# A diffusion block on one core: waits for row copies a block later, vector steps a slice sooner, and the down stage's first slices begun with the other token tile

## The chip, the cores and the metric

The kernel runs on one core of a Trainium2 chip. The metric is the device time of one execution in microseconds (us), as a median over runs. The core has a matrix engine (TensorE; PE in the profile, with its weight loads apart as PEld), a vector engine (VectorE, DVE), an activation engine (ScalarE, ACT), GpSimd (POOL) and SyncE (SP). They run their own instruction streams side by side and meet at semaphores. Matmul results lie in PSUM, eight banks of 128 x 512 floats; everything else lies in SBUF.

## What is computed

Two layers of a diffusion backbone over 256 latent tokens of width 2048. Layer 0 mixes tokens by attention (with 256 context tokens), layer 1 by a two-dimensional Fourier transform. Each mixer is followed by a squared-ReLU MLP of inner width 8192, and each sub-layer is normalised, shifted and scaled, and gated, by vectors that are products of SiLU(c) with a 2048 x 12288 matrix:

```python
mod_lat = (silu_c @ ada_w[i] + ada_b[i])[:, None, :]
sh1, sc1, g1, sh2, sc2, g2 = jnp.split(mod_lat, N_MOD, axis=-1)
...
x = x + g1 * o_lat
x = x + g2 * sq_relu_mlp(modulate(rms_norm(x, norm_mlp_g[i]), sh2, sc2), mlp_w1[i], mlp_w2[i])
...
return rms_norm(x, final_norm_g)
```

All is float32. The change touches the MLP of both layers and the modulation vectors that are worked out beside it.

## The kernel before

**Precision.** Each weight tile is split in two parts that TensorE reads in one pass each: ScalarE copies `raw` to `w_hi` (`split_hi`, line 496), VectorE subtracts to get `w_lo` (`split_lo`, line 887). A *slice* is 128 x 1024 weights. Four slices lie ready (`SPLIT`); the split of slice s + 4 waits until TensorE has finished slice s (`slice_done`), and VectorE's part comes behind ScalarE's (`hi_ready`, then `lo_ready`). SyncE loads pairs of slices, 1 MB each, into a ring of three.

**Up.** 16 blocks of 8 slices (s = 0 to 127). `up_slice` runs 8 pairs of matmuls for each slice, one of 512 columns (line 1574) and one of 256 (line 1576). A block fills four PSUM banks, odd blocks banks 4 to 7, even blocks banks 0 to 3. Behind a block ScalarE copies one half of its banks to `u` (`b_half`, line 804), then VectorE adds the other half (`add_halves`, line 1327), which sets `ab_ready` and frees the banks; then ScalarE makes the squared ReLU.

**Down.** 128 slices, two to each of 64 row tiles k of `mlp_w2`. `rows_slice` multiplies a slice with token tile 0 (banks 4 to 7) and then token tile 1 (banks 0 to 3), two banks and so 6 matmuls for each (lines 1530, 1533, 1534). Its first slices wait for the last block's `add_halves(15)`, since block 15 used banks 4 to 7.

**Modulation vectors.** VectorE builds vector v in 16 steps, `ada_step(v, t)`, each a 128 x 2048 multiply-add into `ada_sum` (line 912; the first, line 910, only multiplies). GpSimd loads the 1 MB that a step reads (line 466) into a ring of two, once the step two before is done. In layer 0's up stage vectors 3, 4 and 5 are built. `step_slices` says behind the split of which slice of VectorE's loop each step stands. At the slices of `turns` TensorE sums the result over the partitions: for vectors 3 and 5 (slices 42 and 122) with `lay_rows` (line 1506), for gates, that is vector 4 (slice 82) and, in layer 1, vector 9 (slice 106), with `turn_row` (line 1522), four matmuls into the four banks that the running block doesn't use. A gate needs its bias first (`add_bias`, line 920, a one-partition add that sets `biased`); ScalarE copies the four banks to `g_row` (line 649, `row_ready`), and TensorE waits for that before it goes on with the next slice.

All order is written by hand: each engine's stream is its program text, with the waits where they stand.

Of the kernel before, what the change touches and what calls it, by code (L numbers as in the profile page):

```python
# [30 lines left out]
KT = D // P  # L31
# [3 lines left out]
FT = D_FF // P  # L35
# [19 lines left out]
ROWS = {0: 0, 4: 1, 6: 2, 9: 3}  # L55
COLS = {3: 0, 5: 1, 7: 2, 8: 3}
LAID = {3: 6, 5: 7}
UP_STEPS = {0: (3, 4, 5), 1: (9,)}
# [4 lines left out]
def step_slices(l):  # L63

    if l == 0:
        return {(0, 44, 85)[j] + (12 * t) // 5: (v, t) for j, v in enumerate(UP_STEPS[0]) for t in range(KT)}
    return {6 * t: (9, t) for t in range(KT)}


def turns(l):  # L70

    return {42: 3, 82: 4, 122: 5} if l == 0 else {106: 9}
# [83 lines left out]
def layer_block(nc, x, c, ctx_in, c_ctx, ada_w, ada_b, norm_mix_g, norm_mlp_g, w_qkv, q_g, k_g, w_o,  # L156
# [144 lines left out]
    row_ready = sem("row_ready")  # L301
# [3 lines left out]
    lo_ready = sem("lo_ready")  # L305
    slice_done = sem("slice_done")
# [34 lines left out]
    ab_ready = sem("ab_ready")  # L341
# [3 lines left out]
    ulo_ready = sem("ulo_ready")  # L345
# [1037 lines left out]
    def _(pe):  # L1383
# [152 lines left out]
        def rows_slice(first, k, half):  # L1536
# [5 lines left out]
                    ins = rows_bank(s, k, tt, nb, k == 0, False)  # L1542
            ins.then_inc(slice_done, 1)

        def rows_last(first, k0):

            for tt in range(2):
                for nb in range(4):
                    pe.wait_ge(lo_ready, first + 2 * k0 + 3 + nb // 2)
                    rows_bank(first + 2 * k0 + nb // 2, k0, tt, nb, False, False, 1 if tt == 1 and nb == 2 else 0)  # L1550
                    ins = rows_bank(first + 2 * k0 + 2 + nb // 2, k0 + 1, tt, nb, False, True, 2 if tt == 1 and nb == 3 else 0)
                    if tt == 0 or nb < 3:
                        ins.then_inc(bank_full, 1)
            ins.then_inc(slice_done, 1)
# [31 lines left out]
        for i in range(8):  # L1586
# [3 lines left out]
            for k in range(2):  # L1590
                for tt in range(2):
                    f = 2 * i + k
                    ins = nc.tensor.transpose(ps[:, i % 4, k * T + tt * P:k * T + (tt + 1) * P], xn_in[:, tt, f * P:(f + 1) * P],
                                              ident[:, :])
# [114 lines left out]
        for l in range(2):  # L1709
# [102 lines left out]
            for blk in range(16):  # L1812
                if blk == 1:
                    pe.wait_ge(hT_ready, 2 * (8 * q + 8))
                if blk >= 2:
                    pe.wait_ge(ab_ready, 16 * l + blk - 1)
                for p in range(8):
                    if blk == 0:
                        if 1 <= p < 5:
                            turn_pair(p + 3)  # L1820
                        pe.wait_ge(hl_ready, 8 * q + p + 1)
                    up_slice(l, blk, p)
                    t = turns(l).get(8 * blk + p)
                    if t is not None:
                        pe.wait_ge(ab_ready, 16 * l + blk)
                        if t in ROWS:
                            turn_row(t, range(4), 4 * ((blk + 1) % 2))
                            pe.wait_ge(row_ready, 4 * ROWS[t] + 4)
                        else:
                            lay_rows(t, 4 * ((blk + 1) % 2))  # L1830
                    t = picks(l).get(8 * blk + p)
                    if t is not None:
                        pick_cols(t, 4 * ((blk + 1) % 2))
                if l == 0 and blk in (5, 15):
                    pe.wait_ge(mod_ready, COLS[(3, 5)[blk // 15]] + 1)

            first = 2 * P_DOWN[l]
            for k in range(FT - 2):
                for half in range(2):
                    if half == 0 and k % 2 == 0:  # L1840
                        pe.wait_ge(ulo_ready, 32 * l + k // 2 + 1)
                    if k == 0:
                        pe.wait_ge(ab_ready, 16 * l + 16)
                    rows_slice(first, k, half)
            pe.wait_ge(ulo_ready, 32 * l + 32)
            rows_last(first, FT - 2)
# [48 lines left out]
```

## Time and profile before

| | us |
|---|---|
| median of 3 runs | 2121.84 |
| lowest and highest | 2119.29, 2124.86 |
| the profiled execution | 2124.03 |
| its span in the trace | 2122.2 |

All positions in the text are microseconds from the start of that span. Layer 0's up stage lies at about 510 to 884 and its down stage behind it; layer 1's up stage lies at about 1389 to 1758. "Idle" of an engine is time before an instruction in which it did nothing; the profile puts it down to the instruction or transfer that ended it.

### The profile page before, as it was taken

How to read it: one execution, taken by the hardware profiler on the slowest of the kernel's cores; microseconds unless marked ns; L12 is line 12 of the kernel's file. 1: busy time of each engine (PE TensorE's matmuls, PEld its weight loads, DVE VectorE, ACT ScalarE, POOL GpSimd, SP SyncE). 2: the span in 40 equal slices, each digit the busy share in tenths (PEclk: the TensorE clock that was granted, in tenths of full speed). 3: DMA queues.
4: the chain of work that ended last, by engine and by line, in shares of the span. 5: the costliest groups of instructions: out<-in, count | busy, mean ns of one | idle time of the engine just before them, and what ended most of it. 6: DMA issues, size and time to landing. Idle time of an engine off the chain costs nothing.

```text
span 2122.2 us, 25347 instructions
## 1 busy us (share of the span) xinstructions
PE 2034.3 (96%) x10468; PEld 1649.6 (78%) x10468; DVE 1344.2 (63%) x1351; ACT 979.0 (46%) x1275; POOL 109.3 (5%) x196
## 2 busy tenths in 40 slices
PE   4999979999999999999999999999999999999997
PEld 3677745567888878788888888878888887888886
DVE  2456876447877867677658867876656544545455
ACT  4433554435554554444444444354544554444443
POOL 1111001000000000000000000000000000000000
PEclk8999989999999999999999999989999999999999
DMA  9798548585988979688669826967777555555653
GB/s 369 267 337 328 197 171 314 197 309 182 356 315 311 357 274 350 217 317 327 247 216 354 344 70 238 365 202 245 243 252 238 188 172 178 197 198 188 211 196 119
DMA packets 150924, 538.90 MB, mean 254 GB/s; under 512 B 8437, under 2 KB 9621, under 8 KB 113301
## 3 DMA queue, kind: packets, MB, share of 16 engines
q1 hardware_dynamic: 116816, 329.73, 44.2%
q0 software_dynamic: 31744, 201.34, 25.6%
q10 hardware_dynamic: 2248, 6.21, 0.8%
q8 instruction: 83, 1.36, 0.3%
q14 instruction: 33, 0.26, 0.0%
HBM read 535.15 MB, written 2.10 MB: 253 GB/s over the span
## 4 chain that ended last, share of the span: by engine, by line
PE 89%; DVE 5%; DMA 3%; ACT 2%; issue 1%; POOL 0%; DVEq 0%; SPq 0%; ACTq 0%; POOLq 0%
PE ps L1574 22%; PE ps L1576 11%; PE ps L1530 11%; PE ps L1533 11%; PE ps L1534 11%; PE ps L1388 5%; PE ps L1389 5%; PE ps L1390 5%; PE ps L1449 1%; PE ps L1429 1%; DVE ada_sum L912 1%; DMA spare<-in_ada_w 1%; PE ps L1700 1%; PE ps L1652 1%; DMA c_rows<-in_ctx 1%
## 5 line engine op out<-in xcount | busy, mean ns | idle before, releaser
L887 DVE TENSOR_TENSOR w_lo<-raw,w_hi 128x1024 fp32r<-128x1024 f32 x624 | 759.5, 1223 | 585.8 <-ACT w_hi L496 585.7
L496 ACT ACTIVATE w_hi<-raw 128x1024 fp32r<-128x1024 f32 x624 | 658.1, 1059 | 902.5 <-PE ps L1534 380.2
L1574 PE MATMUL ps<-hh,w_hi 128*128 128x512 f32 x2048 | 723.4, 399 | 4.6 <-DVE hh L1208 3.3
L1576 PE MATMUL ps<-hh,w_lo 128*128 128x256 f32 x2048 | 573.5, 280 | 0.0
L1574 PEld LDWEIGHTS ps<-hh,w_hi 128*128 128x128 f32 x2048 | 386.1, 189 | 101.9 <-issue 4.8
L1530 PE MATMUL ps<-w_hi,hh 128*128 128x512 f32 x1024 | 400.0, 391 | 5.0 <-DVE u L1327 2.6
L1533 PE MATMUL ps<-w_lo,hh 128*128 128x512 f32 x1024 | 399.8, 390 | 0.0
L1534 PE MATMUL ps<-w_hi,hh 128*128 128x512 f32 x1024 | 399.5, 390 | 0.0
L1576 PEld LDWEIGHTS ps<-hh,w_lo 128*128 128x128 f32 x2048 | 387.6, 189 | 0.0
L912 DVE SCALAR_TENSOR_TENSOR ada_sum<-ada_raw,silu,ada_sum 128x2048 f32<-128x2048 f32 x98 | 229.8, 2345 | 3.6 <-DMA ada_raw<-in_ada_w 3.6
L1530 PEld LDWEIGHTS ps<-w_hi,hh 128*128 128x128 f32 x1024 | 192.9, 188 | 46.1 <-issue 6.0
L1534 PEld LDWEIGHTS ps<-w_hi,hh 128*128 128x128 f32 x1024 | 193.1, 189 | 40.4
L1533 PEld LDWEIGHTS ps<-w_lo,hh 128*128 128x128 f32 x1024 | 193.0, 189 | 39.8
L1388 PE MATMUL ps<-w_hi,hh 128*128 128x512 f32 x448 | 195.6, 436 | 16.2 <-DVE hh L1006 9.6
L1389 PE MATMUL ps<-w_lo,hh 128*128 128x512 f32 x448 | 177.6, 397 | 0.0
L1390 PE MATMUL ps<-w_hi,hh 128*128 128x512 f32 x448 | 177.1, 395 | 0.0
L466 POOL DMA_DIRECT2D ada_raw<-in_ada_w x132 | 69.8, 529 | 1230.0 <-DVE ada_sum L912 738.1
L1388 PEld LDWEIGHTS ps<-w_hi,hh 128*128 128x128 f32 x448 | 85.9, 192 | 60.4 <-issue 37.1
L1389 PEld LDWEIGHTS ps<-w_lo,hh 128*128 128x128 f32 x448 | 86.0, 192 | 23.3 <-issue 7.7
L1390 PEld LDWEIGHTS ps<-w_hi,hh 128*128 128x128 f32 x448 | 85.6, 191 | 19.0
L1352 DVE TENSOR_TENSOR hh<-u,hh 128x512 fp32r<-128x512 f32 x64 | 43.4, 683 | 0.0
L1327 DVE TENSOR_TENSOR u<-ps,u 128x1024 f32<-128x1024 f32 x32 | 39.0, 1218 | 6.5 <-ACT u L804 6.5
(180 smaller groups left out, 1320.4 us busy)
## 6 DMA issues: line engine op xcount, KB each, us to landing
raw<-in_mlp_w SPq DMA_DIRECT2D x256, 1024.0 KB, 5.3
ada_raw<-in_ada_w POOLq DMA_DIRECT2D x151, 1024.0 KB, 5.8
spare<-in_ada_w POOLq DMA_DIRECT2D x32, 1024.0 KB, 7.5
raw<-in_attn_w_qkv SPq DMA_DIRECT2D x24, 1024.0 KB, 9.9
raw<-in_attn_w_o SPq DMA_DIRECT2D x16, 1024.0 KB, 7.2
raw<-in_fourier_w_o SPq DMA_DIRECT2D x16, 1024.0 KB, 5.6
g_row<-in_ada_w POOLq DMA_DIRECT2D x9, 1024.0 KB, 10.0
x_tm<-in_x ACTq DMA_DIRECT2D x2, 1024.0 KB, 7.6
```

Source lines behind the costliest of these rows:

```text
L466: pool.dma_start(ring(vector_slot(i)), ada_v[lay][m, i % KT]).then_inc(ada_in[vector_slot(i)], 16)
L496: act.activation(w_hi[:, s % SPLIT, :], raw[:, piece % RAW, s % 2, :], ACT.Copy).then_inc(hi_ready, 1)
L887: nc.vector.tensor_tensor(w_lo[:, s % SPLIT, :], raw[:, s // 2 % RAW, s % 2, :], w_hi[:, s % SPLIT, :].bitcast(F32), ALU.subtract).then_in ...
L912: ins = nc.vector.scalar_tensor_tensor(sum_of(v)[:, :], ring(slot), col, sum_of(v)[:, :], ALU.mult, ALU.add)
L1388: mm(dst, w_h, m_h, start=start, stop=False, skip_group_check=True)
L1389: mm(dst, w_h, m_l, start=False, stop=False, skip_group_check=True)
L1390: return mm(dst, w_l, m_h, start=False, stop=stop, skip_group_check=True)
L1530: ins = mm(bank_of(tt, nb), h_hi[:, k % KT, tok], w_hi[:, s % SPLIT, cols], start=start, stop=False)
L1533: mm(bank_of(tt, nb), h_hi[:, k % KT, tok], w_lo[:, s % SPLIT, cols], start=False, stop=False)
L1534: return mm(bank_of(tt, nb), h_lo[:, k % KT, tok], w_hi[:, s % SPLIT, cols], start=False, stop=stop)
L1574: mm(ps[:, bank, :].rearrange("p (a t) -> p a t", a=2), w_hi[:, s % SPLIT, w], hh[:, k, :, :], start=(k == 0), stop=False, skip_group_chec ...
L1576: ins = mm(ps[:, bank, 0:T], w_lo[:, s % SPLIT, w], h_hi[:, k, :], start=False, stop=(k == KT - 1), skip_group_check=True)
```

## The change

Three edits. `step_slices`: vector 4 begins a slice sooner (43 for 44) at the same spacing, so that its last step stands at slice 79 and not 80; vector 5 begins a slice sooner (84 for 85) and takes a step every 11/5 slices for 12/5, so that its last step stands at slice 117 and not 121. In up, TensorE's wait for `row_ready` moves from behind `turn_row` to the start of the next block. In down, the first two slices (k = 0) are done by a new function, `rows_first`: token tile 1 of both slices first, which only needs block 14's banks, then the wait for `add_halves(15)`, then token tile 0 of both. No work is added or taken away.

```diff
-        return {(0, 44, 85)[j] + (12 * t) // 5: (v, t) for j, v in enumerate(UP_STEPS[0]) for t in range(KT)}
+        return {(0, 43, 84)[j] + ((12, 12, 11)[j] * t) // 5: (v, t) for j, v in enumerate(UP_STEPS[0]) for t in range(KT)}
...
+        def rows_first(l, first):
+
+            pe.wait_ge(ulo_ready, 32 * l + 1)
+            pe.wait_ge(ab_ready, 16 * l + 15)
+            for tt in (1, 0):
+                if tt == 0:
+                    pe.wait_ge(ab_ready, 16 * l + 16)
+                for half in range(2):
+                    if tt == 1:
+                        pe.wait_ge(lo_ready, first + half + 1)
+                    for nb in (2 * half, 2 * half + 1):
+                        ins = rows_bank(first + half, 0, tt, nb, True, False)
+                    if tt == 0:
+                        ins.then_inc(slice_done, 1)
...
+                for t in range(8 * blk - 8, 8 * blk):
+                    if turns(l).get(t) in ROWS:
+                        pe.wait_ge(row_ready, 4 * ROWS[turns(l)[t]] + 4)
...
                             turn_row(t, range(4), 4 * ((blk + 1) % 2))
-                            pe.wait_ge(row_ready, 4 * ROWS[t] + 4)
...
-            for k in range(FT - 2):
+            rows_first(l, first)
+            for k in range(1, FT - 2):
                 for half in range(2):
                     if half == 0 and k % 2 == 0:
                         pe.wait_ge(ulo_ready, 32 * l + k // 2 + 1)
-                    if k == 0:
-                        pe.wait_ge(ab_ready, 16 * l + 16)
```

In what follows `up_slice`'s two lines, 1574 and 1576, are 1589 and 1591 in the changed kernel.

VectorE in layer 0's up stage, around the end of vector 4; line 1327 is `add_halves(9)`, 912 the last steps, 920 the bias. Before:

```order
L887 TENSOR_TENSOR w_lo<-raw,w_hi 128x1024 x2
L1327 TENSOR_TENSOR u<-ps,u 128x1024
L887 TENSOR_TENSOR w_lo<-raw,w_hi 128x1024
L912 SCALAR_TENSOR_TENSOR ada_sum<-ada_raw,silu,ada_sum 128x2048
L920 TENSOR_TENSOR ada_sum<-ada_sum,g_row 1x2048
L887 TENSOR_TENSOR w_lo<-raw,w_hi 128x1024 x5
L910 TENSOR_SCALAR ada_sum<-ada_raw,silu 128x2048
```

The same place in the changed kernel:

```order
L887 TENSOR_TENSOR w_lo<-raw,w_hi 128x1024 x3
L912 SCALAR_TENSOR_TENSOR ada_sum<-ada_raw,silu,ada_sum 128x2048
L920 TENSOR_TENSOR ada_sum<-ada_sum,g_row 1x2048
L1327 TENSOR_TENSOR u<-ps,u 128x1024
L887 TENSOR_TENSOR w_lo<-raw,w_hi 128x1024 x5
L910 TENSOR_SCALAR ada_sum<-ada_raw,silu 128x2048
```

The last step and the bias now stand ahead of `add_halves(9)` and of one split.

TensorE at the same turn, slice 82 and the start of slice 83, with the waits that an instruction carries. Before:

```order
L1576 MATMUL ps<-hh,w_lo 128x256
L1522 MATMUL ps<-ada_sum,ones 128x512 [waits biased,ab_ready]
L1522 MATMUL ps<-ada_sum,ones 128x512 x3
L1574 MATMUL ps<-hh,w_hi 128x512 [waits lo_ready,row_ready]
L1576 MATMUL ps<-hh,w_lo 128x256
```

And in the changed kernel:

```order
L1591 MATMUL ps<-hh,w_lo 128x256
L1522 MATMUL ps<-ada_sum,ones 128x512 [waits biased,ab_ready]
L1522 MATMUL ps<-ada_sum,ones 128x512 x3
L1589 MATMUL ps<-hh,w_hi 128x512 [waits lo_ready]
L1591 MATMUL ps<-hh,w_lo 128x256
```

The wait for `row_ready` is gone from slice 83; it stands on the first matmul of slice 88.

TensorE at the start of down, from the seventh matmul on (layer 0), as the difference of before (-) and after (+):

```order
-L1530 MATMUL ps<-w_hi,hh 128x512 [waits lo_ready,ab_ready]
+L1530 MATMUL ps<-w_hi,hh 128x512 [waits lo_ready]
+L1533 MATMUL ps<-w_lo,hh 128x512
+L1534 MATMUL ps<-w_hi,hh 128x512
+L1530 MATMUL ps<-w_hi,hh 128x512
+L1533 MATMUL ps<-w_lo,hh 128x512
+L1534 MATMUL ps<-w_hi,hh 128x512
+L1530 MATMUL ps<-w_hi,hh 128x512 [waits ab_ready]
```

The wait for `add_halves(15)` (`ab_ready`) now stands behind twelve matmuls; before, the very first matmul carried it.

## Rows read from the trace of the kernel before

**Rows 1.** The page: busy time by engine; the chain that ended last, by engine
```profile
PE 2034.3 (96%) x10468; PEld 1649.6 (78%) x10468; DVE 1344.2 (63%) x1351; ACT 979.0 (46%) x1275; POOL 109.3 (5%) x196
...
PE 89%; DVE 5%; DMA 3%; ACT 2%; issue 1%; POOL 0%; DVEq 0%; SPq 0%; ACTq 0%; POOLq 0%
```
**Rows 2.** Timeline, layer 0's gate (slice 82): start, duration, engine, line, [idle, releaser]
```profile
737.71 1.22 DVE L887 TENSOR_TENSOR w_lo<-raw,w_hi 128x1024 fp32r<-128x1024 f32 x1 [0.92 <-ACT w_hi L496]
738.86 1.22 DVE L1327 TENSOR_TENSOR u<-ps,u 128x1024 f32<-128x1024 f32 x1
...
741.63 2.34 DVE L912 SCALAR_TENSOR_TENSOR ada_sum<-ada_raw,silu,ada_sum 128x2048 f32<-128x2048 f32 x1
...
744.01 2.28 DVE L920 TENSOR_TENSOR ada_sum<-ada_sum,g_row 1x2048 f32<-1x2048 f32 x1
...
744.56 0.28 PE L1576 MATMUL ps<-hh,w_lo 128*128 128x256 f32 x1
746.44 3.67 PE L1522 MATMUL ps<-ada_sum,ones 128*128 128x512 f32 x8 [1.59 <-DVE ada_sum L920]
750.80 0.50 PE L1574 MATMUL ps<-hh,w_hi 128*128 128x512 f32 x1 [0.69 <-ACT g_row L649]
```
**Rows 3.** Timeline, layer 1's gate (slice 106)
```profile
1694.90 3.59 PE L1522 MATMUL ps<-ada_sum,ones 128*128 128x512 f32 x8
...
1699.18 0.50 PE L1574 MATMUL ps<-hh,w_hi 128*128 128x512 f32 x1 [0.69 <-ACT g_row L649]
```
**Rows 4.** Timeline, vector 5's rows (slice 122)
```profile
863.85 0.28 PE L1576 MATMUL ps<-hh,w_lo 128*128 128x256 f32 x1
...
866.13 1.06 PE L1506 MATMUL ps<-ada_sum,ones 128*32 128x512 f32 x8 [2.00 <-DVE ada_sum L912]
```
**Rows 5.** Timeline, start of down in layer 0
```profile
880.21 2.35 DVE L887 TENSOR_TENSOR w_lo<-raw,w_hi 128x1024 fp32r<-128x1024 f32 x2
...
883.44 0.28 PE L1576 MATMUL ps<-hh,w_lo 128*128 128x256 f32 x1
...
884.82 1.22 DVE L1327 TENSOR_TENSOR u<-ps,u 128x1024 f32<-128x1024 f32 x1 [2.25 <-ACT u L804]
...
886.30 0.47 PE L1530 MATMUL ps<-w_hi,hh 128*128 128x512 f32 x1 [2.57 <-DVE u L1327]
...
888.55 0.63 PE L1534 MATMUL ps<-w_hi,hh 128*128 128x512 f32 x1
888.98 0.63 PE L1530 MATMUL ps<-w_hi,hh 128*128 128x512 f32 x1
889.20 1.23 DVE L887 TENSOR_TENSOR w_lo<-raw,w_hi 128x1024 fp32r<-128x1024 f32 x1 [2.03 <-ACT w_hi L496]
```
**Rows 6.** Timeline, start of down in layer 1
```profile
1757.41 0.28 PE L1576 MATMUL ps<-hh,w_lo 128*128 128x256 f32 x1
1760.12 0.47 PE L1530 MATMUL ps<-w_hi,hh 128*128 128x512 f32 x1 [2.42 <-issue]
```
**Rows 7.** Stretches: A:B length, busy us and (instructions) by engine, PEclk, DMA share, GB/s
```profile
631.00:650.00 19.00, 19.00 (x114) 15.74 (x113) 10.29 (x10) 8.71 (x9) 0.55 (x2) 1.00 0.66 222
864.13:871.00 6.87, 4.87 (x22) 3.53 (x22) 2.99 (x2) 1.92 (x3) 0.53 (x1) 0.75 0.94 336
883.72:891.40 7.68, 5.11 (x17) 4.08 (x17) 4.18 (x4) 6.13 (x7) 0.00 (x0) 0.78 0.32 132
1757.69:1765.20 7.51, 5.09 (x16) 4.07 (x16) 4.18 (x4) 6.35 (x7) 0.00 (x0) 0.77 0.15 64
693.20:737.60 44.40, 44.40 (x257) 38.81 (x257) 36.89 (x25) 22.64 (x24) 3.70 (x7) 1.00 0.97 353
788.90:834.10 45.20, 45.20 (x257) 39.17 (x257) 35.49 (x25) 22.57 (x24) 3.70 (x7) 1.00 0.96 346
1790.00:1820.00 30.00, 30.00 (x134) 24.86 (x133) 15.28 (x14) 13.30 (x15) 0.00 (x0) 1.00 0.54 181
```
**Rows 8.** Loads of the vectors' weights, 755 to 860
```profile
DMA to landing us min/median/max: 5.3/5.9/9.7
```

## The prediction

> **What bounds the kernel now.** I read the page first: TensorE is busy for 96% of the span and makes up 89% of the chain that ended last [rows 1]. So only time in which TensorE stands, or runs below its speed, can be won; work that is moved on other engines is worth nothing by itself. Next I went through TensorE's stream at the places that the diff names, to see in front of which instruction it stands and what ended that. The reader should look at the square brackets. At layer 0's gate it stands twice, 1.59 us for VectorE's bias add and 0.69 us for ScalarE's last row copy [rows 2]; at layer 1's gate only for the copy, 0.69 us [rows 3]; at slice 122, 2.00 us for VectorE's last step [rows 4]; at the start of down 2.57 us for VectorE's `add_halves(15)` in layer 0 [rows 5] and 2.42 us in layer 1, where the profile names no releaser, but the code has the same wait [rows 6]. Last I took the stretches, for the clock and the pace [rows 7].
>
> **The gate in layer 0.** Matmuls of this stream start 0.11 us after the start of the last 256-column one where nothing is waited for: in layer 1 `turn_row` begins so at 1694.90 [rows 3]. So `turn_row` could begin at 744.56 + 0.11 = 744.67 and begins at 746.44: 1.77 us [rows 2]. What is in its way after the change? VectorE's loop of slice 79 ends its split at about 738.86 (737.71, where the next instruction then starts). The order now is last step, bias, `add_halves(9)`: from 738.86 the step runs to 741.2, the bias (it starts 0.03 behind the step) to 743.5, `add_halves` to 744.6 to 744.7, all with the durations of [rows 2]. `biased` is in time by 1.1 us. `ab_ready` of block 9, which the same instruction waits for, now comes last, about when TensorE arrives or 0.1 us later. I book 1.65. The split that falls behind both is of slice 84, which TensorE reads some 6 us later; nothing else waits for it.
>
> The wait for `row_ready`: the last of the eight records of `turn_row` ends at 750.11 and slice 83 starts at 750.80 [rows 2], so 0.7 us goes here and 0.7 in layer 1 [rows 3]. At the next block's start, five slices later, the copies are long over. ScalarE's copies don't slow: they read banks that block 10 doesn't write. The split behind them waits for the end of slice 83, at 744.7 + 3.7 + 2.8 = 751.2, and the last copy is then over by some 2 us, since it ends just ahead of 750.80 today and moves up by 1.65. Sum: 1.65 + 0.7 + 0.7 = 3.05.
>
> **Slice 122.** `lay_rows` could begin at 863.85 + 0.11 = 863.96 and begins at 866.13: 2.17 us [rows 4]. The last step now stands 4 slices (11 us) ahead, so this wait goes wholly.
>
> **Start of down.** Without a wait the first matmul would stand at 883.44 + 0.11 = 883.55 for 886.30: 2.75 us; in layer 1 at 1757.52 for 1760.12: 2.60 us [rows 5, 6]. `rows_first` fills that gap with 12 matmuls. Down runs 134 of them in 30.00 us, 0.224 us each [rows 7], so 12 last 2.7 us, to 886.25. `add_halves(15)` ends at 884.82 + 1.22 = 886.04 [rows 5], and today TensorE starts 0.26 later. So the cover fits, with nothing to spare: if it misses, it misses by a tenth or so. What is late next? The third slice's split follows `add_halves`, 1.2 us more, and ends at about 887.2; TensorE wants it at 883.55 + 24 x 0.224 = 888.9. The fourth ends at 889.20 + 1.23 = 890.4 [rows 5] and is wanted at 891.6. So the gap doesn't come back. `slice_done` of the first slice comes after 18 matmuls for 12, 887.6; the split that it frees is held by ScalarE's own queue until later. Sum: 5.35, less 0.1 for the fit: 5.25.
>
> **The clock.** Behind three of these waits the granted clock drops to its lower level, 1.2 GHz: the mean is 0.75, 0.78 and 0.77 over the stretches that hold them [rows 7], and the matmuls of down stand 0.43 us apart (888.55, 888.98) [rows 5] for 0.224. Missing clock is 0.25 x 6.87, 0.22 x 7.68 and 0.23 x 7.51, about 1.7 us each, 3.4 us at half speed; as the spacing falls only from 0.43 to 0.224, a drop costs 3.4 x (1 - 0.224/0.43) = 1.6 us. The bounds are 0 (the drop comes whether or not TensorE waits) and 1.7. I take 1.6 for all three: at slices 42 to 45 `lay_rows` and its followers run with no wait ahead, and there the clock stays at 1.00 (the first row of [rows 7]), so the light matmuls alone don't do it. Sum: 4.8.
>
> The Trainium skill, page "TensorE: Matmul & The Clock Gate", section "Why this matters for your kernels", asks only that longer idle gaps than these be kept out for the clock to stay up. By that rule the waits are not what lowers it, the 4.8 us would stay, and the gain would be 10.5; the rows, where each drop stands right behind such a wait, are on the other side.
>
> **The denser steps.** Vector 5's steps want 1 MB each 2.2 slices. A block is 22.2 to 22.6 us and carries 4.2 MB of weights; with steps at 12/5 it carries 3.5 MB more, with 11/5 3.8 MB, so the demand rises from 346 to about 360 GB/s. 353 is moved over 44 us at a DMA share of 0.97 [rows 7]. A load may be asked for once the step two before is done, four slices ahead at the least: 4 x 2.77 - 2.35 for that step = 8.7 us; loads land in 5.3 to 9.7 us, median 5.9 [rows 8]. A single late load makes VectorE wait about 1 us, and the splits queued behind it, but TensorE has some 6 us of splits in hand (the split behind slice s is done about 2.3 us after its end and is wanted three slices, 8.3 us, after it). So I book 0, bounds 0 and 1. VectorE itself has room: 35.49 of 45.20 us busy [rows 7]; 0.3 more steps a block add 0.7 us.
>
> The Trainium skill's page "DMA: Bandwidth & Descriptors", section "Where 436 GB/s comes from", gives about 358 GB/s as what memory feeds one core. By that figure 33 slices at 360 would run under 1% late, an estimate of 0.6 us; no stretch of these rows stands far enough above it to settle that.
>
> **The pace.** Up runs at two paces at the same clock of 1.00: 257 matmuls in 44.40 us or in 45.20 [rows 7], 0.80 us for 16 slices, 0.05 a slice. It changes at the interruptions (fast up to slice 82, slow behind it), I can't say by what rule. The change alters how slices 83 to 121 and 107 to 127 are entered: the first may turn fast (2.0 us less), the second slow (1.1 more). I book 0 for the even chance and keep both ends.
>
> **Sum.** 3.05 + 2.17 + 5.25 + 4.8 = 15.3. The profiled execution took 2124.03, so it would take 2108.8; it lies 2.2 above the median of 2121.84, for which I forecast 2106.6. Own range: 2103.5 to 2109.
>
> **Rivals.**
> - *The clock drops anyway*, or at other places: TensorE's four light matmuls at slice 122 and the start of down stay. The gain is 10.5, the time 2111.3. For it speaks only that a wait of 1.59 us at the gate left the clock at 1.00; against it, the row without a wait. 0.12.
> - *New waits take over*: `add_halves(9)` now sits behind a step and a bias of 4.6 us, and a late load for that step would push `ab_ready` past TensorE's arrival by as much; with `add_halves(15)` late too, 2 to 5 us of the 8 of waits remain and one drop with them: 2110 to 2113. The fits of 0.1 us speak for it, the equal durations of all these records against it. 0.07.
> - *The change doesn't do what it says in down*: TensorE stands before its first matmul for something else (the splits of the first two slices, `ulo_ready`). Those splits end at 882.56 [rows 5], a microsecond before TensorE comes, so 0.01; 2114.
> - *Slower*: vector 5's loads can't keep the denser beat. VectorE's splits stand behind each waiting step, so TensorE then runs at the speed of the loads. Two steps take one landing and about 3 us; at 11/5 that must fit in 12.2. With landings of L each, eight pairs lose 8 x (L + 3 - 12.2), less 6 in hand. It eats the 15.3 at L = 11.9 us and is slower by 0.3% at 12.7; at 14 it gives 2106.6 + 32 = 2139. The longest landing was 9.7 and the median 5.9 [rows 8], so 0.03.
>
> **The numbers.** The forecast has 0.77, the rivals 0.12, 0.07, 0.01 and 0.03. A change of 0.3%, 6.4 us, is about what a measurement of this kernel can tell from none: faster than 2115.5 holds for all cases but the last; with a margin for what I don't see (the pace of layer 1's whole up stage, 106 slow slices and so 5 us, may fall otherwise in a run, as the runs from 2119.29 to 2124.86 suggest) 0.91; same 0.06, slower 0.03. The range reaches from the fast pace, 2106.6 - 4, to the two rivals at 2113.
>
> **What would show it.** In the changed trace: no idle ahead of `turn_row`, `lay_rows` of slice 122, the slices behind the gates, and the first matmul of down; at most 0.2 us ahead of its 13th; the clock at 1.00 from 864 to 892 on the old scale and at down's start in layer 1. The last step of vector 5 ends some 11 us ahead of `lay_rows`. Wrong would be: idle ahead of down's 13th or 25th matmul, VectorE waiting on a load of more than 1 us, a lower clock with no wait ahead, or a total gain under 10.

## The result: 19.7 us less at first, 15 us less on two more chips

| | median us | lowest to highest | runs |
|---|---|---|---|
| before | 2120.57 | 2115.77 to 2124.86 | 6 |
| changed | 2100.85 | 2098.13 to 2109.72 | 6 |
| ratio | 0.9909, 95% interval 0.989 to 0.9929 | | |

The changed kernel is 19.7 us faster (0.9%). 2106.6 was forecast, in a range from 2102.6 to 2113.0, so the median lies 1.75 us below the range. The execution that was profiled took 2109.72, the slowest of the six. It has a span of 2107.9 for 2122.2 before: 14.3 us less, where the sum of the prediction was 15.3. So the trace of this execution can show whether the terms were right, but not where the last four microseconds of the median come from.

TensorE is busy for as large a share as before, and as much of the chain is its own [rows 1]. It is a kernel with the same limit, less some waiting. The page of the changed kernel:

```profile
PE 2029.2 (96%) x10468; PEld 1646.9 (78%) x10468; DVE 1343.9 (64%) x1351; ACT 978.6 (46%) x1275; POOL 109.3 (5%) x196
...
PE 89%; DVE 5%; DMA 3%; ACT 2%; issue 1%; POOL 0%; DVEq 0%; SPq 0%; ACTq 0%; POOLq 0%
```

What TensorE waits for in layer 0's up stage and the start of down (500 to 900; us in total, times, longest). Both lines are the start of the stage, which the change doesn't touch; the bias, the row copy, the last step and `add_halves(15)` are gone:

```profile
PE ps L1576 <- DVE xn L1200: 3.4, 1, 3.4
PE ps L1589 <- DVE hh L1208: 1.5, 1, 1.5
```

**Layer 0's gate** (answers to [rows 2]), TensorE and then VectorE in the changed kernel:

```profile
746.83 0.28 PE L1591 MATMUL ps<-hh,w_lo 128*128 128x256 f32 x1
746.97 3.70 PE L1522 MATMUL ps<-ada_sum,ones 128*128 128x512 f32 x8
750.11 0.80 PE L1589 MATMUL ps<-hh,w_hi 128*128 128x512 f32 x1
750.74 0.28 PE L1591 MATMUL ps<-hh,w_lo 128*128 128x256 f32 x1
...
743.50 2.28 DVE L920 TENSOR_TENSOR ada_sum<-ada_sum,g_row 1x2048 f32<-1x2048 f32 x1
745.71 1.20 DVE L1327 TENSOR_TENSOR u<-ps,u 128x1024 f32<-128x1024 f32 x1
```

`turn_row` starts 0.14 behind the start of the slice's last matmul; before it was 1.88. `add_halves(9)` ends at 746.91, 0.06 before `turn_row` begins: it is what comes last now, as the prediction had it. The next slice's first matmul is drawn from 750.11, before the modelled end of `turn_row` (746.97 + 3.70); for a clean comparison take the second one. From the slice's last matmul to it were 751.13 - 744.56 = 6.57 us, and now 750.74 - 746.83 = 3.91: 2.66 us gained. The 751.13 is the second of these two rows of the kernel before; the fourth belongs to layer 1's gate, the third to slice 122:

```profile
750.80 0.50 PE L1574 MATMUL ps<-hh,w_hi 128*128 128x512 f32 x1 [0.69 <-ACT g_row L649]
751.13 0.28 PE L1576 MATMUL ps<-hh,w_lo 128*128 128x256 f32 x1
...
867.12 0.68 PE L1574 MATMUL ps<-hh,w_hi 128*128 128x512 f32 x1
...
1699.52 0.28 PE L1576 MATMUL ps<-hh,w_lo 128*128 128x256 f32 x1
```

**Slice 122** (to [rows 4]) **and layer 1's gate** (to [rows 3]) in the changed kernel:

```profile
863.46 0.28 PE L1591 MATMUL ps<-hh,w_lo 128*128 128x256 f32 x1
863.67 1.06 PE L1506 MATMUL ps<-ada_sum,ones 128*32 128x512 f32 x8
864.66 0.50 PE L1589 MATMUL ps<-hh,w_hi 128*128 128x512 f32 x1
...
1685.82 3.59 PE L1522 MATMUL ps<-ada_sum,ones 128*128 128x512 f32 x8
1688.85 0.79 PE L1589 MATMUL ps<-hh,w_hi 128*128 128x512 f32 x1
1689.48 0.27 PE L1591 MATMUL ps<-hh,w_lo 128*128 128x256 f32 x1
```

Around slice 122 it is 867.12 - 863.85 = 3.27 before and 1.20 now: 2.07 gained. In layer 1, from `turn_row` to the second matmul behind it, 4.62 before and 3.66 now: 0.96.

**The start of down** (to [rows 5] and [rows 6]), layer 0 and then layer 1:

```profile
879.42 0.28 PE L1591 MATMUL ps<-hh,w_lo 128*128 128x256 f32 x1
879.54 0.39 PE L1530 MATMUL ps<-w_hi,hh 128*128 128x512 f32 x1
...
880.80 1.23 DVE L1327 TENSOR_TENSOR u<-ps,u 128x1024 f32<-128x1024 f32 x1 [2.26 <-ACT u L804]
...
882.06 0.39 PE L1534 MATMUL ps<-w_hi,hh 128*128 128x512 f32 x1
882.29 0.40 PE L1530 MATMUL ps<-w_hi,hh 128*128 128x512 f32 x1
...
1747.37 0.28 PE L1591 MATMUL ps<-hh,w_lo 128*128 128x256 f32 x1
1747.49 0.39 PE L1530 MATMUL ps<-w_hi,hh 128*128 128x512 f32 x1
```

Down begins 0.12 behind up's last matmul: 2.86 - 0.12 = 2.74 gained in layer 0, and 2.71 - 0.12 = 2.59 in layer 1. The matmul at 882.29 is the 13th, the first that needs `add_halves(15)`, which ends at 880.80 + 1.23 = 882.03. It starts 0.23 behind the 12th, at down's own beat: the fit of a tenth held. The five places together give 2.66 + 0.96 + 2.07 + 2.74 + 2.59 = 11.0 us, where 10.5 was forecast.

**The clock and the new demand** (to [rows 7]). The same three stretches in the changed kernel hold a granted clock of 1.00 throughout (the third figure from the end of a line, ahead of the DMA share), for 0.75, 0.78 and 0.77 before; the last line is the load on DMA while vector 5 is built, 770 to 850:

```profile
863.67:870.54 6.87, 6.87 (x42) 5.31 (x42) 2.45 (x2) 4.49 (x7) 0.00 (x0) 1.00 0.46 155
879.70:887.38 7.68, 7.68 (x36) 6.31 (x35) 4.54 (x5) 7.26 (x8) 0.00 (x0) 1.00 0.33 128
1747.65:1755.16 7.51, 7.51 (x34) 6.17 (x34) 4.38 (x5) 7.10 (x8) 0.00 (x0) 1.00 0.15 63
...
770.00:850.00 80.00, 80.00 (x454) 69.42 (x454) 65.73 (x45) 40.34 (x40) 6.90 (x13) 1.00 0.97 358
```

### The profile page after: what moved, and what is told of

Same layout as the page of the kernel before. It is cut to its first block, busy times and chain, and to the rows that moved or that the text cites. A ratio compares the mean times of both kernels' runs of the same rounds, so it can differ in the third digit from the quotient of the medians.

```text
span 2107.9 us, 25343 instructions
## 1 busy us (share of the span) xinstructions
PE 2029.2 (96%) x10468; PEld 1646.9 (78%) x10468; DVE 1343.9 (64%) x1351; ACT 978.6 (46%) x1275; POOL 109.3 (5%) x196
## 4 chain that ended last, share of the span: by engine, by line
PE 89%; DVE 5%; DMA 3%; ACT 2%; issue 1%; POOL 0%; DVEq 0%; SPq 0%; ACTq 0%; POOLq 0%
PE ps L1589 23%; PE ps L1591 11%; PE ps L1530 11%; PE ps L1533 11%; PE ps L1534 11%; PE ps L1388 5%; PE ps L1389 5%; PE ps L1390 5%; DMA ada_raw<-in_ada_w 1%; PE ps L1449 1%; DMA spare<-in_ada_w 1%; DVE ada_sum L912 1%; PE ps L1429 1%; PE ps L1715 1%; PE ps L1667 1%
## 5 line engine op out<-in xcount | busy, mean ns | idle before, releaser
L1388 PE MATMUL ps<-w_hi,hh 128*128 128x512 f32 x448 | 193.6, 432 | 16.8 <-DVE hh L1006 11.0
```

What stands on the lines that cost most here:

```text
L1388: mm(dst, w_h, m_h, start=start, stop=False, skip_group_check=True)
```

## The experiments

Twelve runs in three groups, each group on a chip of its own, beside the kernel before. e1 to e4 are the first group, e5 to e8 the second, e9 to e12 the third. That kernel's medians were 2123.15 (17 runs), 2122.64 (17) and 2121.58 (11).

### One part at a time

`e1_down_only` is the kernel before with `rows_first`; the steps and the wait for `row_ready` stay as they were. `e2_up_only` is the changed kernel with the old start of down. First e1 against the changed kernel, then e2:

```diff
-        return {(0, 43, 84)[j] + ((12, 12, 11)[j] * t) // 5: (v, t) for j, v in enumerate(UP_STEPS[0]) for t in range(KT)}
+        return {(0, 44, 85)[j] + (12 * t) // 5: (v, t) for j, v in enumerate(UP_STEPS[0]) for t in range(KT)}
...
-                for t in range(8 * blk - 8, 8 * blk):
-                    if turns(l).get(t) in ROWS:
-                        pe.wait_ge(row_ready, 4 * ROWS[turns(l)[t]] + 4)
...
+                            pe.wait_ge(row_ready, 4 * ROWS[t] + 4)
```

```diff
-            rows_first(l, first)
-            for k in range(1, FT - 2):
+            for k in range(FT - 2):
...
+                    if k == 0:
+                        pe.wait_ge(ab_ready, 16 * l + 16)
```

> The kernel before with the new start of down alone; up stays as it was. Theory (each wait of TensorE is worth its idle time, and with it goes the drop of the clock behind it): 2.75 - 0.1 + 1.6 us in layer 0 and 2.6 + 1.6 in layer 1, so 8.5 us less than before at the same pace of up, about 0.4%. No lower clock at the two starts of down; still one behind slice 122 of layer 0. Rival (the clock drops anyway): 5.3 us less, and a stretch at 1.2 GHz right behind each start of down. Rival for the 2 to 4 us by which the whole change beat the forecast: if they come from down, this kernel is 11 us or more faster.

> The changed kernel with down's old start: the earlier steps of the vectors and the moved waits alone. Theory: 1.65 + 0.7 + 0.7 + 2.17 + 1.6 = 6.8 us less than before at the same pace of up, 0.3%; the two starts of down keep their waits of 2.4 to 2.6 us and the lower clock behind them. Rival (the surplus over the forecast comes from up): 10 us or more, with fewer slices of up at the slow pace than in before, in every profile and in the median of the runs. If the pace is chance, its slow slices are some other number than the changed kernel's 176.

Measured: e1 2116.49 (2108.86 to 2121.86, 12 runs), 0.9969 of the kernel before, interval 0.9956 to 0.9981: 6.7 us less. e2 2110.51 (2106.59 to 2115.92, 6 runs), 0.995, interval 0.9934 to 0.9966: 12.6 us less. The two add up to 19.3, as much as the change as a whole gave at first. But by the terms of the prediction down was to give 5.25 of waits and 3.2 of clock, 8.5, and up 5.2 and 1.6, 6.8: down gave less and up nearly twice as much. For e2 that is the size the rival wanted (10 us or more), but without its sign, fewer slow slices: e2 has 181 of them for 143 before, as the table further down shows. What TensorE waits for from 500 to 900, in e1 and then in e2:

```profile
PE ps L1506 <- DVE ada_sum L912: 2.0, 1, 2.0
PE ps L1522 <- DVE ada_sum L920: 1.6, 1, 1.6
PE ps L1589 <- ACT g_row L649: 0.7, 1, 0.7
...
PE ps L1530 <- DVE u L1327: 2.6, 1, 2.6
```

So each part takes away its own waits and leaves the other's. The surprise is the clock behind those that are left. Stretches of the same lengths as in [rows 7], e1's slice 122 and then e2's two starts of down:

```profile
863.90:870.77 6.87, 4.88 (x31) 3.56 (x31) 2.99 (x2) 2.60 (x4) 0.53 (x1) 1.00 0.92 340
...
879.38:887.06 7.68, 5.11 (x23) 4.25 (x24) 4.56 (x5) 6.58 (x7) 0.00 (x0) 1.00 0.34 129
1746.60:1754.11 7.51, 5.09 (x23) 4.24 (x23) 4.38 (x5) 6.51 (x7) 0.00 (x0) 1.00 0.13 53
```

The wait is there (TensorE works for 2.0, 2.6 and 2.4 us less than the stretch lasts), and the clock stays at 1.00. Here the account of the prediction (a wait of this length brings a drop of 1.6 us) is wrong, at least as a rule.

### How often does the clock drop behind these waits?

`e6_before_again` and `e12_before_look` are the kernel before, unaltered.

> The kernel before once more, for its second profile. The same theory: time less 0.053 us for each slow slice and 0.47 us for each us of low clock is within 1 us of 2075.6, so 10.8 above the changed kernel's. Its runs on this chip had a median of 2123, which by the theory needs some 200 slow slices. Rival: the count is as in the first profile, 140, and the time is high for another reason.

> The kernel before, one look at the clock. The three waits that the prediction charged with a clock drop each are slice 122's (2.0 us) and those at down's two starts (2.6 and 2.4). Theory (a drop behind such a wait is chance): at least one of the three has the clock at 1.00 behind it, as two of three had in the last look at this kernel. Rival (in the kernel before the wait does cause it, and the last look was the exception): 0.75 to 0.78 behind all three, as in the first profile.

Measured: e6 2122.85 (2118.32 to 2127.62, 12 runs), 1.0005 of the kernel before beside it, interval 0.9994 to 1.0016; e12 took 2121.84. The same three stretches in e6 and then in e12:

```profile
866.32:873.19 6.87, 4.88 (x30) 3.57 (x31) 2.98 (x2) 2.61 (x4) 0.53 (x1) 1.00 0.92 336
884.60:892.28 7.68, 5.12 (x16) 4.07 (x17) 4.18 (x4) 5.72 (x7) 0.00 (x0) 0.78 0.32 129
1756.58:1764.09 7.51, 5.09 (x23) 4.24 (x23) 4.37 (x5) 6.51 (x7) 0.00 (x0) 1.00 0.13 57
...
865.84:872.71 6.87, 4.86 (x30) 3.55 (x30) 3.00 (x2) 2.61 (x4) 0.53 (x1) 1.00 0.93 341
884.14:891.82 7.68, 5.11 (x16) 4.06 (x17) 4.18 (x4) 5.72 (x7) 0.00 (x0) 0.78 0.33 128
1755.53:1763.04 7.51, 5.09 (x15) 4.12 (x16) 4.18 (x4) 5.96 (x7) 0.00 (x0) 0.77 0.12 50
```

One drop behind three waits, and two behind three. With the first profile's three and none in e1 and e2 that makes 6 drops behind 12 waits: 1 of 4 at slice 122, 3 of 4 at the start of down in layer 0, 2 of 4 in layer 1. The other side matters as much: the nine profiles of kernels with all three waits removed (the change three times and the six kernels below), with e1's two starts of down and e2's slice 122, make 30 such places without a wait, and in none of them did the clock drop. So the wait does make the drop, but only about every second time (6 of 12 for 0 of 30; what decides between the two is not shown). Of the two expectations for e12 the first held, that a drop is chance.

### The change on two more chips

`e5_change_again` and `e9_change_third` are the changed kernel, unaltered.

> The changed kernel once more, for a second profile and more runs beside the kernel before. In the first profile it shows 176 slices of up in clear stretches at the slow pace and took 2109.7, while its other five runs took 2098 to 2103. Theory (waits 10.5 us, and the rest of a run's time set by how many slices are slow, 0.053 us each, and by how long the clock is low, 0.47 us for each): in this profile the time less those two terms is within 1 us of 2065, as it is for the first profile, and if the run is near 2100 it shows few slow slices. Rival (the runs differ by something else, such as transfers): a run near 2100 shows as many slow slices as the first.

> The change, unaltered, on one more chip, beside the next three kernels. Theory (the change is worth 15 us of waits and clock; the 19.7 of the first measurement held some 4 us of chance in how the few runs were drawn): 13 to 18 us below the kernel before. Rival (19.7 is its true worth and the 15.3 of the second chip was the chance): 19 to 20 on this chip again. In its profile the theory wants the third stretch without any of the named waits, and the slices of layer 1's up stage up to 106 slow, since they were so in all profiles but the one with the four small matmuls.

Measured: e5 2107.37 (2102.25 to 2107.61, 5 runs), 0.9919, interval 0.9904 to 0.9934: 15.3 us less. e9 2106.08 (2102.61 to 2109.07, 6 runs), 0.9927, interval 0.9913 to 0.9942: 15.5 less. Both lie within a microsecond of the forecast. The named waits are gone in both traces. The stretch of layer 1's up stage was slow in both, as expected.

All 17 executions of the change in order: 2098.13, 2098.56, 2099.85, 2101.85, 2102.25, 2102.61, 2103.06, 2103.34, 2103.45, 2104.67, then a gap, 2107.37, 2107.45, 2107.48, 2107.61, 2107.87, 2109.07, 2109.72. Their mean is 2104.4; that of 45 executions of the kernel before on the three chips of the experiments is 2122.3. Those two means mix the chips unequally. Chip by chip the mean gain is 18.5 in the first measurement, 17.0 beside e5 and 15.1 beside e9, 16.8 over the 17 executions. And a median of five or six from such a row jumps by several microseconds, depending on which side of the gap its middle falls.

What can differ from one execution to the next? Two things stand in the traces, the time at the lower clock and the pace of up. To take both out: a matmul of down costs 0.224 us at the upper clock and 0.43 at the lower [rows 5, 7], so each microsecond at 1.2 GHz costs 1 - 0.224/0.43 = 0.48. The 16 matmuls of an up slice take 2.66 us from the first start to the last at the fast pace and 2.70 to 2.72 at the slow one; with the seam it is 0.054 a slice. Counting both in every trace, within its span:

| profile | span us | us at 1.2 GHz | slow slices of some 255 | span less both |
|---|---|---|---|---|
| before | 2122.2 | 84.2 | 143 | 2074.1 |
| e6, before | 2119.4 | 71.4 | 182 | 2075.4 |
| e12, before | 2120.0 | 82.2 | 100 | 2075.2 |
| e1, down alone | 2111.0 | 65.4 | 182 | 2069.8 |
| e2, up alone | 2109.5 | 61.4 | 181 | 2070.3 |
| changed | 2107.9 | 72.5 | 179 | 2063.5 |
| e5, changed | 2100.4 | 61.8 | 142 | 2063.1 |
| e9, changed | 2106.1 | 67.8 | 145 | 2065.7 |

The last column should differ by the waits alone. It falls from 2074.9 in the mean to 2064.1: 10.8 us, where the five places gave 11.0 in the trace above and 10.5 was forecast. Down alone gives 5.1 (forecast 5.25) and up alone 4.6 (5.22). Traces of one kernel differ in it by 1.3 to 2.6 us, so these figures hold to about a microsecond. The expectations for e5 and e6 asked for this measure within 1 us of the first trace of the same kernel: e5 met it, e6 came out 1.3 above. Its 182 slow slices are near the 200 that its theory wanted; e5, the fastest traced, has 142 and 10.7 us less lower clock than the first trace, so its theory held in part. What made e1's gain small and e2's large lies in the other two columns and in how few executions a median rests on, not in the waits. The rest of the 15.7 us between the mean spans, 2120.5 and 2104.8, is 11.9 us less time at the lower clock, so 5.7, less 0.7 for 14 more slow slices (within the rounding).

### What sets the pace?

The prediction could not say. Layer 1's up stage (slices 1 to 106) has 106 slices in a row, 5.7 us between the two paces, and the same place shows both. The stretch from 1420 to 1680 at a clock of 1.00 in the changed kernel, then in e12: 1473 and 1501 matmuls in the same 260 us:

```profile
1420.00:1680.00 260.00, 260.00 (x1473) 225.44 (x1472) 157.65 (x119) 129.51 (x126) 6.36 (x12) 1.00 0.70 235
...
1420.00:1680.00 260.00, 260.00 (x1501) 227.39 (x1501) 160.97 (x122) 132.67 (x129) 6.34 (x12) 1.00 0.71 243
```

The pace changes only where something other than up's pairs runs on TensorE. `e3_nudge4` adds four matmuls of 4 columns behind slice 10 in both layers and slice 84 in layer 0; `e10_nudge4_again` is the same kernel on another chip. `e4_each_block` adds one such matmul in each of layer 1's blocks 1 to 12. Nothing reads their results:

```diff
+        def nudge(bank, n):
+            for f in range(n):
+                mm(ps[:, bank, 4 * f:4 * f + 4], ident[:, :], ones[:, 0:4], start=True, stop=True)
...
+                    if 8 * blk + p in ((10, 84), (10,))[l]:
+                        pe.wait_ge(ab_ready, 16 * l + blk)
+                        if l == 0 and blk == 10:
+                            pe.wait_ge(row_ready, 4 * ROWS[4] + 4)
+                        nudge(4 * ((blk + 1) % 2), 4)
```

> The changed kernel with three added interruptions of up: four matmuls of 4 columns, results unused, behind slices 10 and 84 of layer 0 and slice 10 of layer 1. They cost about 0.9 us each, 2.7 in all. Theory A (the pace of up is set at each entry into the stream, and such short matmuls, as those behind slice 45 in both traces, set the fast one): all slices behind the three places run at the fast pace, 0.05 us each less, so this kernel's profile shows under 20 slow slices, all its runs lie close together, and its time is about 2098.5 + 2.7 = 2101, whatever the pace at the stage's start. Theory B (the pace belongs to the place in the stage, by banks, data or transfers): slices 84 to 121 of layer 0 and 11 to 105 of layer 1 stay slow in the profile, and the time is 2.7 us above the changed kernel's. Theory C (chance at every entry): about half of the stretches turn fast.

> The changed kernel with one matmul of 4 columns, result unused, behind the third slice of each of blocks 1 to 12 of layer 1's up stage: twelve entries in one trace. It costs 12 x 0.3 to 0.6 us. Theory A (set at the entry): the pace can differ from block to block, and if the interruption always sets the same one, all twelve stretches show it. Theory B (by place): blocks 1 to 12 are all slow, as in both traces. Theory C (chance at each entry): a mixture, about half and half, with no order.

> The change with four 4-column matmuls (results unused) behind slice 10 of each layer and behind slice 84 of layer 0, a second time. Theory that an interruption draws the pace anew by chance: layer 1's slices 11 to 105 may be at either pace, and the four runs of the pace at the nudges need not repeat. Rival (the interruption fixes the pace by its place and kind): the same pattern as the first time, layer 1's slices 11 to 105 fast and layer 0's 83 to 121 slow, and a time of 0.05 x 60, so 3 us, below the change on the same chip.

Measured: e3 2103.61 (2101.05 to 2106.18, 5 runs), 0.9915, interval 0.99 to 0.993. e10 2103.84 (2102.49 to 2106.38, 4 runs), 0.9921, interval 0.9907 to 0.9935. e4 2109.84 (2108.88 to 2110.69, 4 runs), 0.9945, interval 0.993 to 0.9961. The stretch from 1420 to 1680 in e3, e10 and e4:

```profile
1420.00:1680.00 260.00, 260.00 (x1498) 228.70 (x1497) 160.47 (x121) 133.36 (x130) 6.37 (x12) 1.00 0.70 238
...
1420.00:1680.00 260.00, 260.00 (x1502) 229.25 (x1501) 160.46 (x122) 131.71 (x129) 6.35 (x12) 1.00 0.70 239
...
1420.00:1680.00 260.00, 260.00 (x1482) 225.81 (x1481) 156.71 (x119) 128.43 (x125) 6.37 (x12) 1.00 0.69 233
```

Four small matmuls at slice 10 turned layer 1 from slow to fast, in both executions. At slice 84 they left a slow stream slow, at layer 0's slice 10 a fast one fast, again in both. So e3 bears out neither its theory A (all fast) nor B (all as before). In every stretch between two interruptions the two executions agree, which speaks against an even draw at each interruption and for place and kind, as far as two executions can. A single small matmul left the slow pace alone twelve times out of twelve (its extra matmuls are in the count of 1482). But without nudges the same kernel does differ: the change enters slice 83 slow in two traces and fast in e5, and the kernel before runs layer 1 fast in one of three. One regularity stands in all eleven traces with the old order of matmuls: behind layer 1's `turn_row` (slice 106) the pace is the other one, slow to fast in eight and fast to slow in three. Behind layer 0's (slice 82), always entered fast, it turns slow in nine and stays fast in two, e5 and e4. 68 slow slices for 145 would be 4.2 us, but each group of four costs 0.9 (the two slices around it take 6.4 to 6.5 us for 5.5 or 5.7), 2.7 in all, so 1.5 is left; e10 came out 2.2 under e9 on the same chip, with ratios of 0.9921 and 0.9927 whose intervals overlap. A kernel that always gains by this was not shown.

`e7_by_four` and `e8_by_eight` take the alternation away. In e7 the four 512-column matmuls of a k come first and then its four of 256 columns, in e8 all eight of a slice and then the eight; `e11_by_eight_again` is e8 on another chip. The edit of e8:

```diff
-            for a in range(2):
-                k = 2 * p + a
-                for j in range(4):
...
+            for low in range(2):
+                for a in range(2):
+                    k = 2 * p + a
+                    for j in range(4):
...
+                        if not low:
+                            mm(ps[:, bank, :].rearrange("p (a t) -> p a t", a=2), w_hi[:, s % SPLIT, w], hh[:, k, :, :], start=(k == 0),
+                               stop=False, skip_group_check=True)
+                        else:
+                            ins = mm(ps[:, bank, 0:T], w_lo[:, s % SPLIT, w], h_hi[:, k, :], start=False, stop=(k == KT - 1),
+                                     skip_group_check=True)
```

> The changed kernel with up_slice's matmuls in another order: for each k the four of 512 columns, then the four of 256, in place of pairs of both. Every bank still adds in the same order. Theory A (the two paces are two phases into which the alternation of sizes locks; down, with one size, shows one pace in all traces): with one change of size in four there is one pace, and if it is the fast one, all 256 slices take 2.77 us, the time less the clock's share is 2065 and the runs keep within the clock's spread: 2096 to 2100. Rival B (the pace isn't about sizes): slow and fast stretches as before. Rival C (four accumulations into four banks with the weight load of another part cost more): one pace, slower than 2.83 us a slice, and 2110 or more.

> As the kernel before it, with all eight matmuls of 512 columns of a slice, then all eight of 256. Theory A: one pace as well, the same as with four or a little faster, since the sizes change only twice a slice. Rival B: two paces. Rival C: slower than 2.83 us a slice.

> The change with the eight 512-column matmuls of a slice first and then the eight 256-column ones, a second time, now beside the change on the same chip for 5 rounds. Its profile had one pace, 2.67 us from first to last of a slice's 16 matmuls, near the fast one of the change (2.66; slow 2.71). Theory: with some 140 to 180 slow slices in the change, it is 140 x 0.04 to 180 x 0.05, so 5 to 9 us less, if nothing is lost at the seams of the slices. Rival (the seams give it back): within 3 us of the change, as the first pair (2106.09 for 2107.37) suggests.

Measured: e7 2109.54 (2103.4 to 2111.42, 6 runs), 0.9931, interval 0.9915 to 0.9948. e8 2106.09 (2103.64 to 2106.84, 4 runs), 0.992, interval 0.9905 to 0.9935. e11 2104.98 (2103.02 to 2107.47, 5 runs), 0.9926, interval 0.9913 to 0.9939. The change on the same chips had 2107.37 and 2106.08, so e7 is 2.2 us above it. The stretch from 1420 to 1680 in e8:

```profile
1420.00:1680.00 260.00, 260.00 (x1489) 228.70 (x1488) 159.23 (x120) 132.50 (x130) 6.35 (x12) 1.00 0.69 236
```

There is one pace now (2.67 us from first to last in e8 and e11, 2.68 to 2.69 in e7), so the two paces belong to the alternation of 512 and 256 columns. But the one pace lies between the old two, 1489 matmuls for 1473 and 1501, and the times of e8 and e11 are 1.1 to 1.3 us under the change, which the intervals don't separate. The expectation of 5 to 9 us fell. Its rival, that the seams give it back, isn't borne out either: from the start of a slice's last matmul to the start of the next slice it is 0.12 us in e8 and e11 as in the change. From the start of one slice to the next they take 2.793 us, for 2.773 at the fast pace and 2.828 at the slow one. With 142 to 179 slow slices in the change that is worth 3 to 5 us, less than booked because 2.793 is not the fast pace. And the clock stood lower: 0.9829 in the mean of the nine executions of e8 and e11, for 0.9847 in the eleven of the change on the same chips, which is 3.9 us of missing full-speed clock and so 3.7 us of time. Whether the order of the matmuls has a part in that is not shown. No kernel tried is clearly better than the change.

## Why the waits came out as forecast and the time fell outside the range, point by point

**The waits.** Every one went, and nothing came in its place. Forecast and measured: gate of layer 0 2.35 and 2.66; gate of layer 1 0.7 and 0.96; slice 122 2.17 and 2.07; down 2.75 - 0.1 and 2.74, and 2.60 and 2.59. The wait for `row_ready` was sized too small, at the idle time of 0.69 [rows 2, 3]: it gave 0.96 in layer 1. The stream behind `turn_row` starts before the end that the profile models for it (750.11 for 750.67), so that idle time is some 0.3 us too small for what the wait cost. The fits of a tenth of a microsecond held, 0.14 for 0.11 at the gate and 0.23 at down's 13th matmul. Vector 5's last step (851.93 to 854.28) ended 9.4 us ahead of `lay_rows`, for some 11 in the forecast, which cost nothing.

**The clock.** Right in size by luck, wrong in kind. I booked three drops of 1.6 us, 4.8, because each stood behind a wait in one trace. By the 12 waits above each comes about half of the time, which makes 2.4: this term was twice too large. Between the three traces of before and the three of the change lie 11.9 us of lower clock, 5.7 us of time, and by the mean clock of the executions beside e5 and beside e9 (0.9823 to 0.9850 and 0.9822 to 0.9845; 6.0 and 5.2 us less missing full-speed clock, each of which costs 0.96) it is 5.8 and 4.9. Of the 11.9 only 6.8 are such drops (six of 3.4 us in three traces, without e1 and e2). The other 5.1, 2.4 us of time, lie elsewhere, in the first 510 us, around 1240 and 1380 and at the end, where it varies from trace to trace. Whether the change has a part in that is open.

The rival that the clock drops anyway fell with 0 of 30. The Trainium skill, page "TensorE: Matmul & The Clock Gate", section "Why this matters for your kernels", which warned only of longer gaps, agrees with 6 of the 12 waits here and not with the other 6.

**The denser steps.** Booked at 0, and nothing is seen. VectorE waits for its loads for 4.6 us in the whole changed trace and for 3.6 before, but all of it lies between 1347 and 1376, behind layer 0's down stage; in layer 0's up stage no step waits for a load in any of the fourteen traces. One of these waits has a TensorE wait of 0.70 us behind it. A wait of over 1 us for a load was named as a sign of being wrong; it stands outside the stage of the denser steps, and the kernel before has one as well. These are the lines of `ada_step` on the pages of before and changed, then its waits in the changed kernel with the one of TensorE, then the longest in the kernel before, and last the stretch from 770 to 850 in e4:

```profile
L912 DVE SCALAR_TENSOR_TENSOR ada_sum<-ada_raw,silu,ada_sum 128x2048 f32<-128x2048 f32 x98 | 229.8, 2345 | 3.6 <-DMA ada_raw<-in_ada_w 3.6
...
L912 DVE SCALAR_TENSOR_TENSOR ada_sum<-ada_raw,silu,ada_sum 128x2048 f32<-128x2048 f32 x98 | 229.8, 2345 | 4.6 <-DMA ada_raw<-in_ada_w 4.6
...
1347.56 2.35 DVE L912 SCALAR_TENSOR_TENSOR ada_sum<-ada_raw,silu,ada_sum 128x2048 f32<-128x2048 f32 x1 [1.48 <-DMA ada_raw<-in_ada_w]
...
1364.74 2.35 DVE L912 SCALAR_TENSOR_TENSOR ada_sum<-ada_raw,silu,ada_sum 128x2048 f32<-128x2048 f32 x1 [3.10 <-DMA ada_raw<-in_ada_w]
...
1367.24 4.59 PE L1499 MATMUL ps<-ones,ada_sum 128*128 128x1 f32 x32 [0.70 <-DVE ada_sum L912]
...
1373.68 2.35 DVE L912 SCALAR_TENSOR_TENSOR ada_sum<-ada_raw,silu,ada_sum 128x2048 f32<-128x2048 f32 x1 [2.29 <-DMA ada_raw<-in_ada_w]
...
770.00:850.00 80.00, 80.00 (x463) 69.94 (x462) 66.59 (x46) 41.13 (x40) 6.90 (x13) 1.00 0.98 365
```

365 GB/s at a DMA share of 0.98: the demand of about 360 was met. The Trainium skill's 358 (page "DMA: Bandwidth & Descriptors", section "Where 436 GB/s comes from", half of what it gives for the memory that two cores share) was passed over 80 us by the one core that runs here, and no wait shows the 0.6 us that I had estimated from it.

**The step that failed: the low end of the range, and in it the term for the pace.** The waits were right within a microsecond, and two of the three measurements fell on the forecast. But the pace was booked at 0 with the ends 2.0 us less (slices 83 to 121) and 1.1 more, and the range's low end was put 4 us under the forecast for "the fast pace", of which the working gives only those 2.0. The text itself named layer 1's up stage, "106 slow slices and so 5 us, may fall otherwise in a run", and used it for the chances alone. The runs showed in its place that layer 1's stretch stands at either pace in one and the same kernel, 5.7 us apart (1473 and 1501 matmuls in 260 us). The text also left out that the time at the lower clock elsewhere moves by up to 11 us from one execution to the next (68 to 75 in the kernel before without the three drops, 62 to 73 in the changed one), so 4 to 5 us of time, and that a median of a handful of executions carries a part of all this. With 5 us for layer 1's pace beside layer 0's 2, the low end would have been about 2100, and the range would have held 2100.85. That the pace made this very median is not shown.

**What stays open.** Ten of the change's 17 executions lie between 2098 and 2105 and seven between 2107 and 2110; the three with a trace were 2102.25, 2107.87 and 2109.72, and layer 1's up stage was slow in all of them. The lowest ones, 2098.13 to 2099.85, weren't traced, but their granted clock is on record. The clock doesn't explain them: 2099.85 has 0.983, just as the traced 2109.72. With 2.0 us taken off for each thousandth of clock, the five untraced executions of the first measurement lie 5.5 to 9.9 us under the traced one (rounding of the clock can make 2 us of that). Layer 1's stretch is 5.7 us, and all 179 slow slices together are 9.7, so in most of the five more than layer 1's stretch would have to be fast. Nor is it shown why the same kernel enters a stretch once fast and once slow. On the two chips with both kernels' clocks on record nothing else is missing: 10.8 of waits with 5.8 and 4.9 of clock make 16.6 and 15.7, and the mean gains are 17.0 and 15.1. The 18.5 of the first measurement rests on six executions of each kernel, whose two means are each uncertain by about 1.7 us.

## What to carry to other kernels

When the matrix engine is the bound, walk through its stream wait by wait and move each wait behind work that is ready anyway: a wait of 2.6 us went by beginning with the tile whose banks were free, and each forecast held to 0.3 us. A thing that stands behind a wait in one trace is not yet its price: look at a second trace of the same kernel, and at the same wait in a kernel with half of the edit, before booking it in full. And what an engine does at two paces by chance belongs into the range, with its longest stretch.

## What the runs showed that I had not expected

- A wait of 2.0 to 2.6 us between matmuls is followed by 3.4 us at 1.2 GHz in 6 of 12 cases; without one at the same places 0 of 30; waits of 1.6 us at the gate 0 of 4.
- Matmuls of 512 and 256 columns in turn run at a clock of 1.00 at one of two paces, 2.66 or 2.70 to 2.72 us from first to last of 16, for a hundred slices on end. It changes only at interruptions; four matmuls of 4 columns at one place turned slow to fast in two executions of two, and one matmul never did, in twelve places. Sorted by size, the same matmuls have one pace, 2.67.
- Behind layer 1's `turn_row` the pace changed over in eleven traces of eleven, whichever it was before.
- The time at the lower clock in one and the same kernel varied from 71 to 84 us in a span of 2120.
